# A tenth expert tile ahead of the router, a busier TensorE while it decides, and the last expert pair in another order

## The chip, the cores and the metric
The kernel runs on one core of one Trainium2 chip. Its time is the device time of one execution in microseconds. The core has five engines that run side by side and meet at semaphores: TensorE (PE; its weight loads are listed as PEld), VectorE (DVE), ScalarE (ACT), GpSimd (POOL) and SyncE (SP), which here mostly issues DMAs. On-chip memory is SBUF; TensorE writes its products to the eight banks of PSUM, B[0] to B[7], 128 partitions of 512 fp32 each.

## The reference
One block of a diffusion backbone over 512 latent tokens of width 1024, with 256 context tokens, all in fp32. First come a Hyena long convolution and an mLSTM side by side, with one output projection (not touched by the change). Then the expert-choice mixture of experts: 16 experts, each of which takes its 64 best tokens.

```
aff = softmax(h2 @ w_router)                # 512 x 16
g, idx = top_k(aff per expert, 64)
a, u  = xs @ w_gate, xs @ w_up              # per expert 64x1024 @ 1024x2048, twice
ye    = (silu(a) * u) @ w_down * g          # per expert 64x2048 @ 2048x1024
y2    = scatter-add of ye onto the 512 tokens
out   = x + g2 * rmsnorm(y2, post_norm2)
```

The weights of one expert are 24 MB (gate, up and down, 8 MB each), all 16 some 403 million bytes, each read once.

## The kernel before
**Tiles and ring.** An expert is cut into 12 tiles of 128 x 4096 fp32 (2048 KB): gate and up in four pairs (256 rows of the inner dimension each, q = 0 to 3), then four of down. Two experts make a pair, so a pair has 24 tiles in the order of `TILES`: g0 u0 g1 u1 g2 u2 g3 u3 d0 d1 d2 d3 of the first expert (tiles 0 to 11) and the same of the second (12 to 23). There are eight pairs. The tiles go to a ring of `NSLOT` = 8 places in SBUF. In the first pair tiles 0 to 7 fill the eight places and tile 8 goes to `yacc`, the 128 x 4096 tensor that later takes the sums; GpSimd clears it once the tile has been used (L503). From then on tile n takes the place of tile n - 8.

**SyncE's order** (L388 to L449). Its queue is in program order and a wait in it holds all that is behind. Tile 0 is issued when the last tile of the input projection has been used, tile 1 after the inverse transforms, tiles 2 and 3 after the mLSTM numerators, then the router weights (L421), tiles 4 to 6 when the output projection is done (`p_w`), tiles 7 and 8 when the logits are done (`p_lg`). Then each later tile waits (`used`) until TensorE has used the tile whose place it takes: tiles 9 to 16 wait for tiles 0 to 7, tile 17 for tile 9, tile 18 for tile 10 and so on.

**Routing** (TensorE L965 to L983, VectorE L1761 to L1795). After the logits: softmax, eight rounds of max and replace on VectorE for the 64 best, threshold, ranks by two small products, and the selection matrices. TensorE has a few small products in it and otherwise waits. Then it gathers the tokens of the first pair by products with the selection matrix (L998) and starts the experts.

**A pair on TensorE** (`expert_pair`, L1002): `gate_up(0)` into banks 0 to 3 (L1038, L1039), the scatter of the pair before it (`scatter`, L1104, two banks in turn, VectorE adds each half row of 512 to `yacc`, L1823), `turn(0, ...)` (transposes of the hidden activations), `down(0)` (L1062, bank 5), `gate_up(1)`, transposes of the affinity-weighted selection (L1081), gather for the next pair, `turn(1, ...)`, `down(1)`. ScalarE makes the silu (L1317), VectorE the product with up (L1830), ScalarE copies the results out (L1322). In the profile a 128x512 fp32 matmul is two records. The last pair has the same order, without the gather.

**Tail.** After `down(1)` of the last pair: copy of the results, eight scatters, each added on VectorE to `yacc`; then per 128 tokens the sum of squares and the root on ScalarE, reciprocal, product with the gate row and sum with the residual on VectorE. The first 128 tokens are finished by ScalarE and GpSimd (L507 to L510), the other three by VectorE (L1877 to L1880). Four output DMAs of 512 KB.

The working tensor `moe` (128 x 6144) holds the inner tensors of the experts from column 0: gathered tokens 0 to 1023, silu 1024 to 2047, hidden to 3071, turned hidden to 4095, results to 5119. Before that its columns serve the mLSTM and small tables of the router.

Of the kernel before, what the change touches and what calls it, by code (L numbers as in the profile page):

```python
# [16 lines left out]
ALU = mybir.AluOpType  # L17
# [4 lines left out]
P = 128  # L22
# [90 lines left out]
def block_kernel(nc, A, out):  # L113
    ctx = ExitStack()
    with ctx:
# [9 lines left out]
        def slot(n, a=0, b=SLOTF):  # L125
# [107 lines left out]
        hdt = moe[:, 3072:4096].rearrange("p (b n) -> p b n", b=2)  # L233
        ye = moe[:, 4096:5120]
# [4 lines left out]
        y3 = yacc[:, :].rearrange("p (c n) -> p c n", c=NLT)  # L239

# [19 lines left out]
        keep = moe[:, 1280:1280 + NSQ * E]  # L260
        mks = moe[:, 1424:1424 + NSQ * E]
# [3 lines left out]
        shp = moe[:, 1024:1152].rearrange("p (k e) -> p k e", k=KD)  # L265
        shs = moe[:, 1152:1168]
# [7 lines left out]
        d_extra = sem("d_extra")  # L274
# [8 lines left out]
                 "v_wra", "v_h2", "v_ry", "a_y0", "g_y0", "a_aft", "v_sub", "v_aft", "v_th", "v_mkt", "v_slot", "v_xs", "v_hid",  # L283
# [55 lines left out]
        def _(sp):  # L339
# [48 lines left out]
            def expert_tile(i, pair):  # L388
                kind, st = TILES[i]
# [4 lines left out]
                if i == NSLOT and first:  # L394
                    dst, loaded = yacc[:, :], d_extra
# [12 lines left out]
            def used(i, pair):  # L408

                kind, st = TILES[i]  # L410
                sp.wait_ge(S["p_dn" if kind == "d" else "p_gu"], 8 * pair + st + 1)
# [9 lines left out]
            sp.dma_start(wr.rearrange("p (a b) e -> p a (b e)", b=2), A["w_router"][0].rearrange("(a p b) e -> p a (b e)", p=P, b=2)).then_inc(d_wr, 16)  # L421
            sp.wait_ge(S["p_w"], len(DONE))
# [16 lines left out]
            for i in range(NTI - NSLOT):  # L439
                used(i, NPAIR - 1)  # L440
                expert_tile(i + NSLOT, NPAIR - 1)

            for c in (1, 2, 0, 3):
                if c:
                    sp.wait_ge(S["v_res"], c)
                else:
                    sp.wait_ge(S["g_y0"], 2)
                sp.dma_start(out[0, c * P:(c + 1) * P, :], y3[:, c, :]).then_inc(d_out, 16)
            sp.wait_ge(d_out, 16 * NLT)  # L449

        @block.gpsimd
        def _(pool):
# [53 lines left out]

            pool.wait_ge(S["a_y0"], 1)  # L507
            g.tensor_tensor(y3[:, 0, :], y3[:, 0, :], g2p[:, :], ALU.mult).then_inc(S["g_y0"], 1)
            pool.wait_ge(S["g_y0"], 1)
            g.tensor_tensor(y3[:, 0, :], y3[:, 0, :], x3[:, 0, :], ALU.add).then_inc(S["g_y0"], 1)  # L510

        @block.tensor
        def _(pe):
# [434 lines left out]

            rows_turned(0)
# [14 lines left out]
            logits(3)  # L964
            pe.wait_ge(S["v_aft"], 1)  # L965
# [6 lines left out]

            pe.wait_ge(S["v_th"], 1)
# [8 lines left out]
            mm(ranks, ones, before, start=False, stop=True).then_inc(S["p_rk"], 1)  # L982
            pe.wait_ge(S["v_slot"], 2)  # L983
# [18 lines left out]
            def expert_pair(jm, first, last):  # L1002

                def ring_tile(kind, st):
                    i = TILES.index((kind, st))
                    if first and i == NSLOT:
                        pe.wait_ge(d_extra, 16)
                        return yacc[:, :]
# [3 lines left out]
                    if not (first and i < NSLOT):  # L1012
                        count = count + (i - 1) // NSLOT
                    pe.wait_ge(d_ring[r], 16 * count)
                    return slot(SLOT_OF[r])

                def gate_up(e2):

                    for q in range(4):
                        wg = ring_tile("g", 4 * e2 + q).rearrange("p (k n) -> p k n", k=2)  # L1020
# [11 lines left out]
                        for k in range(2):  # L1032
                            lhs = xst[:, 2 * q + k, CAP * e2:CAP * (e2 + 1)]
                            for n in range(4):
                                cols = slice(n * CH, (n + 1) * CH)
                                flags = dict(start=(q == 0 and k == 0), stop=(q == 3 and k == 1))
# [13 lines left out]
                def down(e2):  # L1050

                    turned = S["v_hdt" if e2 else "a_hdt"]
                    for q in range(4):
# [6 lines left out]
                        for k in range(4):  # L1060
                            for half in range(2):
                                x = mm(B[5][CAP * half:CAP * (half + 1), :],  # L1062
                                       hdt[:, q // 2, k * P + at:k * P + at + CAP],
# [11 lines left out]
                turn(0, 1)  # L1075
                down(0)

                gate_up(1)
                pe.wait_ge(S["g_sel"], 2 * jm + 4)
                for c in range(NLT):  # L1080
                    x = tr(B[4][:, c * P:(c + 1) * P], pw[:, c, :], idn)  # L1081
                x.then_inc(S["p_pwt"], 1)
                if not last:
                    pe.wait_ge(S["v_sel"], 4 * jm + 12)
                    if not first:
                        pe.wait_ge(S["v_yacc"], 8 * jm + 8)
                    gather_half(jm, 1)
                pe.wait_ge(S["a_pwt"], jm + 2)
                turn(1, 0)
                if not last:  # L1090
                    gather_half(jm, 0)
                turn(1, 1)
                down(1)

# [17 lines left out]
            scatter(NPAIR - 1, range(2 * NLT))  # L1112

        @block.scalar
        def _(act):
# [195 lines left out]
            def expert_pair(j, last):  # L1311
# [6 lines left out]

                def results(e2):
                    act.wait_ge(S["p_dn"], 8 * j + 4 * e2 + 4)  # L1320
                    for half in range(2):
# [4 lines left out]
                for m in range(2):  # L1326
                    act.wait_ge(S["p_ht"], 4 * j + m + 1)
                    a.activation(hdt[:, m, :], B[3 if m else 4][:, :], ACT.Copy).then_inc(S["a_hdt"], 1)
                results(0)
# [572 lines left out]
```

## Time and profile before
| | us |
|---|---|
| runs | 1377.02, 1379.55, 1380.71; median 1379.55 |
| profiled execution | 1377.64, of which 1375.4 span |
| TensorE busy | 1230.3 (89%) |
| VectorE / ScalarE / GpSimd busy | 309.5 / 186.7 / 35.2 |
| DMA read from HBM | 453.53 MB |
| chain of waits: TensorE / DMA | 61% / 30% of the span |
| largest single entry of the chain | DMA ring<-in_w_exp_up, 28% |
| expert tiles, issue to landing (median) | 25.2 (gate), 27.9 (up), 27.0 (down) |

TensorE's busy time is a poor sign of what bounds this kernel: its records overlap and are modelled. The reader should look for who waits for whom in each stretch: before 410 us the projections and the two token mixers, 410 to 434 the routing, then the experts, and from 1350 the tail. The granted clock is given as a share of 2.4 GHz, 0.50 being 1.2 GHz.

### The profile page before, as it was taken

To read this page: it belongs to the slowest core of one execution; us is meant where nothing else is said; L and a number is where in the kernel's file an instruction comes from. 1 tells how busy PE (TensorE), PEld (TensorE's weight loads), DVE (VectorE), ACT (ScalarE), POOL (GpSimd) and SP (SyncE) were. 2 spreads that over 40 slices of the span, in tenths; PEclk is the share of its full clock that TensorE was granted. 3 is DMA by queue.
4 is the path that set the end of the run, shared out by engine and by line. 5 is a ranking of instruction groups with operands and counts; after the bars stand their busy time and mean duration, and the time that the engine had idled before them with its cause. 6 is when DMAs were issued, how large, how long until landed. Compare 5 with 4: busy or idle time off the path is not lost.

```text
span 1375.4 us, 12966 instructions
## 1 busy us (share of the span) xinstructions
PE 1230.3 (89%) x5360; PEld 534.3 (39%) x5360; DVE 309.5 (23%) x601; ACT 186.7 (14%) x377; POOL 35.2 (3%) x58
## 2 busy tenths in 40 slices
PE   6899999999996999989798988989989898897985
PEld 2444454456463334325234332423423433242331
DVE  3634301737333101201111020110102002010215
ACT  3400010013330101102001010100101101010102
POOL 2000010000000100000000000000000000000001
PEclk9999999999997999999999999999999999999998
DMA  9733422262216999999999999999999999999991
GB/s 352 274 122 122 147 97 94 91 243 99 89 71 280 425 428 428 427 428 427 427 429 429 428 428 428 430 428 428 428 428 430 428 428 428 428 432 426 427 417 63
DMA packets 44504, 456.08 MB, mean 332 GB/s; under 512 B 6048, under 2 KB 6160, under 8 KB 16570
## 3 DMA queue, kind: packets, MB, share of 16 engines
q1 hardware_dynamic: 43826, 455.46, 79.3%
q8 instruction: 23, 0.38, 0.1%
q10 hardware_dynamic: 264, 0.11, 0.0%
q0 software_dynamic: 384, 0.07, 0.0%
q14 instruction: 7, 0.06, 0.0%
HBM read 453.53 MB, written 2.10 MB: 331 GB/s over the span
## 4 chain that ended last, share of the span: by engine, by line
PE 61%; DMA 30%; DVE 5%; issue 2%; ACT 2%; SPq 1%; DVEq 0%; ACTq 0%
DMA ring<-in_w_exp_up 28%; PE B L1062 16%; PE B L666 6%; PE B L1038 6%; PE B L1039 6%; PE B L899 4%; PE B L990 4%; PE B L758 3%; PE B L1104 2%; PE B L825 2%; PE B L716 2%; DMA ring<-in_pos 2%; PE B L1047 1%; PE B L576 1%; PE B L615 1%
## 5 line engine op out<-in xcount | busy, mean ns | idle before, releaser
L1038 PE MATMUL B<-ring,moe 128*64 128x512 f32 x1024 | 468.8, 612 | 78.2 <-DMA ring<-in_w_exp_up 65.6
L1039 PE MATMUL B<-ring,moe 128*64 128x512 f32 x1024 | 467.3, 613 | 0.0
L1038 PEld LDWEIGHTS B<-ring,moe 128*64 128x64 f32 x1024 | 141.0, 141 | 234.9 <-issue 213.6
L1062 PE MATMUL B<-ring,moe 128*64 128x512 f32 x1008 | 220.6, 595 | 0.0
L1830 DVE TENSOR_TENSOR moe<-moe,B 64x512 f32<-64x512 f32 x64 | 43.8, 685 | 734.3 <-ACT moe L1317 733.0
L1039 PEld LDWEIGHTS B<-ring,moe 128*64 128x64 f32 x1024 | 140.9, 141 | 146.3 <-issue 146.3
L1062 PEld LDWEIGHTS B<-ring,moe 128*64 128x64 f32 x1008 | 71.1, 137 | 138.2 <-issue 136.2
L1317 ACT ACTIVATE moe<-B 64x512 f32<-64x512 f32 x64 | 37.9, 592 | 503.5 <-PE B L1039 502.3
L666 PE MATMUL B<-ring 128*128 128x512 f32 x192 | 84.1, 595 | 0.0
L1104 PE MATMUL B<-moe 128*128 128x512 f32 x128 | 64.4, 618 | 9.8 <-DVE yacc L1823 7.9
L990 PE MATMUL B<-moe,xl 128*128 128x128 f32 x448 | 55.0, 281 | 0.0
L990 PEld LDWEIGHTS B<-moe,xl 128*128 128x128 f32 x448 | 53.9, 196 | 0.0
L666 PEld LDWEIGHTS B<-ring 128*128 128x128 f32 x192 | 35.9, 190 | 45.9 <-issue 45.8
L1322 ACT ACTIVATE moe<-B 64x512 f32<-64x512 f32 x32 | 18.9, 592 | 244.5 <-PE B L1062 244.1
L1823 DVE TENSOR_TENSOR yacc<-yacc,B 128x512 f32<-128x512 f32 x64 | 43.8, 684 | 29.1 <-PE B L1104 28.7
L758 PE MATMUL B<-ring 128*128 128x512 f32 x96 | 41.8, 593 | 0.0
L1104 PEld LDWEIGHTS B<-moe 128*128 128x128 f32 x128 | 20.9, 189 | 48.2 <-DVE yacc L1823 34.6
L899 PE MATMUL B<-ring,fr 128*128 128x512 f32 x64 | 28.4, 597 | 0.2 <-ACT fr L1265 0.2
L825 PE MATMUL B<-ring 128*128 128x512 f32 x64 | 28.4, 597 | 0.0
L716 PE MATMUL B<-ring 128*128 128x512 f32 x64 | 28.1, 596 | 0.0
L899 PE MATMUL B<-ring 128*128 128x512 f32 x64 | 28.0, 592 | 0.0
L758 PEld LDWEIGHTS B<-ring 128*128 128x128 f32 x96 | 18.0, 190 | 22.4 <-issue 22.4
(303 smaller groups left out, 790.8 us busy)
## 6 DMA issues: line engine op xcount, KB each, us to landing
ring<-in_w_exp_gate SPq DMA_DIRECT2D x64, 2048.0 KB, 25.2
ring<-in_w_exp_up SPq DMA_DIRECT2D x64, 2048.0 KB, 27.9
ring<-in_w_exp_down SPq DMA_DIRECT2D x63, 2048.0 KB, 27.0
ring<-in_w_mod SPq DMA_DIRECT2D x12, 2048.0 KB, 8.2
ring<-in_w_in SPq DMA_DIRECT2D x6, 2048.0 KB, 7.9
ring<-in_w_out SPq DMA_DIRECT2D x2, 2048.0 KB, 7.8
xl<-in_x SPq DMA_DIRECT2D x1, 2048.0 KB, 21.6
ring<-in_pos SPq DMA_DIRECT2D x1, 2048.0 KB, 26.1
```

The lines of the kernel that those rows point to most:

```text
L666: x = mm(B[b][:, :], w[:, k, m * P:(m + 1) * P], ht[:, k, LC:], start=(k == 0), stop=(k == KD - 1))
L716: x = mm(B[b][:, :], w[:, k, m * P:(m + 1) * P], ht[:, k, LC:], start=(k == 0), stop=(k == KD - 1))
L758: x = mm(B[b][:, :], ht[:, k, t * P:(t + 1) * P], w[:, k, :], start=(k == 0), stop=(k == KD - 1))
L825: x = mm(B[b][:, :], ht[:, k, LC + c * P:LC + (c + 1) * P], w[:, k, :], start=(k == 0), stop=(k == KD - 1))
L899: x = mm(B[b][:, :], lhs, wo[half][:, k, :], start=(k == 0), stop=(k == KD - 1))
L990: x = mm(B[6 + g][:, k * P:(k + 1) * P], x3[:, c, pair_rows(dk)], psel[:, c, :], start=(c == 0), stop=(c == NLT - 1))
L1038: mm(gate, lhs, wg[:, k, cols], **flags)
L1039: x = mm(up, lhs, wu[:, k, cols], **flags)
L1062: x = mm(B[5][CAP * half:CAP * (half + 1), :], hdt[:, q // 2, k * P + at:k * P + at + CAP], wd[:, k, half * CH:(half + 1) * CH], start=(q ...
L1104: mm(B[6 + half][:, :], pwt[:, c, :], ye[:, half * CH:(half + 1) * CH], start=True, stop=True).then_inc(S["p_sca"], 1)
L1823: v.tensor_tensor(dst, dst, B[6 + half][:, :], ALU.add).then_inc(S["v_yacc"], 1)
L1830: v.tensor_tensor(hid[o, n // 2, :], sil[o, n // 2, :], B[n][o, :], ALU.mult).then_inc(S["v_hid"], 1)
```

## The change
- **Tenth tile.** `OWN_HOME` gives two tiles of the first pair a place of their own: tile 7 in columns 1024 to 5119 of `moe`, tile 8 in `yacc`. Tile 7 is issued right behind the router weights, once the mLSTM's last readers of these columns are done (`p_num` 16, `v_hn` 4); tile 9 is issued with tile 8 after the logits, into the place that tile 7 had. Tiles 10 to 16 wait for tiles 0 to 6, tile 17 for tile 9 as before. The router's small tables move from `moe` to `fr`.
- **keep_busy.** 128x512 products whose result nobody reads: one before the wait for the softmax, seven before the wait for the threshold, two before the wait for the slots.
- **Last pair.** Order `LAST`: the 16 gate and up tiles first, then the eight down tiles. The second expert's turned hidden goes to its own columns (`hdl`). Within `gate_up(1)` TensorE turns the selection and puts `yacc` into PSUM by products with the identity (`accumulator`), half row by half row; the rest of these follow later.
- **Tail.** The scatters accumulate in eight banks on top of that; nothing is added on VectorE. ScalarE squares straight from PSUM, VectorE multiplies with the gate row from PSUM and ends each 128 tokens with one fused operation. VectorE copies half of the last results. GpSimd has no part. The last 128 tokens leave in two DMAs.

```
+        OWN_HOME = {NSLOT - 1: moe[:, 1024:5120], NSLOT: yacc[:, :]}
+        LAST = [t for t in TILES if t[0] != "d"] + [t for t in TILES if t[0] == "d"]
+        SCATTER_BANK = [6, 7, 0, 1, 2, 4, 3, 5]
-            return i if first and i < NSLOT else (i - 1) % NSLOT
+            return i if first and i < NSLOT - 1 else (i - 2) % NSLOT
...
             sp.dma_start(wr.rearrange(...), ...).then_inc(d_wr, 16)
+            sp.wait_ge(S["p_num"], NH * NLT)
+            sp.wait_ge(S["v_hn"], NLT)
+            expert_tile(NSLOT - 1, 0)
             sp.wait_ge(S["p_w"], len(DONE))
             expert_tile(4, 0)
             expert_tile(5, 0)
             expert_tile(6, 0)
             sp.wait_ge(S["p_lg"], NLT)
-            expert_tile(7, 0)
             expert_tile(NSLOT, 0)
-            for i in range(NSLOT):
+            expert_tile(NSLOT + 1, 0)
+            for i in range(NSLOT - 1):
                 used(i, 0)
-                expert_tile(i + NSLOT + 1, 0)
+                expert_tile(i + NSLOT + 2, 0)
...
+            def keep_busy(b, n):
+                take(b)
+                for _ in range(n):
+                    mm(B[b][:, :], idn, cst[:, 0:CH], start=True, stop=True)
             logits(3)
+            keep_busy(0, 1)
             pe.wait_ge(S["v_aft"], 1)
...
+            keep_busy(0, 7)
             pe.wait_ge(S["v_th"], 1)
...
+            keep_busy(2, 2)
             pe.wait_ge(S["v_slot"], 2)
...
+                if last:
+                    gate_up(1)
+                    pe.wait_ge(S["a_pwt"], jm + 2)
+                    turn(1, 0)
+                    accumulator(2)
+                    accumulator(3)
+                    turn(1, 1)
+                    down(0)
+                    down(1)
+                    return
...
+            def accumulator(n):
+                c, half = divmod(n, 2)
+                mm(B[SCATTER_BANK[n]][:, :], idn, y3[:, c, half * CH:(half + 1) * CH], start=True, stop=False)
...
-            scatter(NPAIR - 1, range(2 * NLT))
+            pe.wait_ge(S["a_ye"], 4 * NPAIR - 1)
+            for n in range(2 * NLT):
+                c, half = divmod(n, 2)
+                if n == 1:
+                    pe.wait_ge(S["v_ye"], 1)
+                if n in (4, 6):
+                    accumulator(n)
+                    accumulator(n + 1)
+                mm(B[SCATTER_BANK[n]][:, :], pwt[:, c, :], ye[:, half * CH:(half + 1) * CH],
+                   start=False, stop=True).then_inc(S["p_sca"], 1)
...
+            for n in range(2 * NLT):
+                c, half = divmod(n, 2)
+                act.wait_ge(S["p_sca"], 8 * (NPAIR - 1) + n + 1)
+                a.activation(sil[:, half, :], B[SCATTER_BANK[n]][:, :], ACT.Square,
+                             accum_out=(sy if half else ss2)[:, c:c + 1]).then_inc(S["a_sy"], 1)
...
+            def gated(c):
+                for half in range(2):
+                    n, h = 2 * c + half, slice(half * CH, (half + 1) * CH)
+                    dve.wait_ge(S["a_sy"], 2 * NLT + n + 1)
+                    link(v.tensor_tensor(y3[:, c, h], B[SCATTER_BANK[n]][:, :], g2p[:, h], ALU.mult))
+            def result(c):
+                dve.wait_ge(S["a_fsd"], c + 1)
+                link(v.reciprocal(ry[:, c:c + 1], sd2[:, c:c + 1]))
+                for h in (slice(0, D),) if c < NLT - 1 else (slice(0, CH), slice(CH, D)):
+                    stt(y3[:, c, h], y3[:, c, h], ry[:, c:c + 1], x3[:, c, h], ALU.mult, ALU.add).then_inc(S["v_res"], 1)
+            gated(0)
+            for c in range(1, NLT):
+                gated(c)
+                result(c - 1)
+            result(NLT - 1)
```

## Rows read from the trace of the kernel before

**Rows 1.** Windows: start:end, length, five engines busy, PEclk, DMA share, GB/s.

```profile
410.00:432.00 22.00, 8.71 (x38) 7.58 (x39) 13.19 (x47) 2.56 (x6) 1.98 (x3) 0.50 0.98 417
...
430.00:435.00 5.00, 5.00 (x31) 4.72 (x31) 0.73 (x2) 0.25 (x1) 0.00 (x0) 0.70 0.29 125
...
480.00:1340.00 860.00, 770.89 (x3576) 309.77 (x3574) 106.92 (x184) 84.67 (x146) 10.25 (x21) 0.98 1.01 428
...
1340.00:1342.00 2.00, 2.00 (x12) 0.70 (x10) 0.00 (x0) 0.00 (x0) 0.00 (x0) 1.00 0.31 131
```

**Rows 2.** Waits of TensorE from 441 to 1345: us in total, times, longest.

```profile
PE B L1038 <- DMA ring<-in_w_exp_up: 65.6, 31, 3.9
```

**Rows 3.** Timeline of SyncE: start us, us (several merged), queue, line, what.

```profile
363.92 0.38 SPq L421 DMA_DIRECT2D ring<-in_w_router  x1
405.35 0.33 SPq L406 DMA_DIRECT2D ring<-in_w_exp_gate  x1
...
412.99 0.33 SPq L406 DMA_DIRECT2D ring<-in_w_exp_up  x1
...
441.77 9.43 SPq L406 DMA_DIRECT2D ring<-in_w_exp_down  x3
...
479.77 0.33 SPq L406 DMA_DIRECT2D ring<-in_w_exp_up  x1
...
493.51 7.67 SPq L406 DMA_DIRECT2D ring<-in_w_exp_down  x4
```

**Rows 4.** Timeline of TensorE in the routing and the first gathers.

```profile
424.37 0.28 PE L975 MATMUL B<-cst_sb,fr 16*128 16x16 f32 x1 [8.46 <-DVE fr L1784]
...
428.85 5.87 PE L998 MATMUL B<-moe,xl 128*128 128x128 f32 x32 [2.42 <-issue]
...
441.66 2.15 PE L998 MATMUL B<-moe,xl 128*128 128x128 f32 x16
```

**Rows 5.** Timeline of TensorE behind the first silu pause.

```profile
471.38 4.92 PE L1062 MATMUL B<-yacc,moe 128*64 128x512 f32 x16
```

**Rows 6.** Timeline of the last pair, TensorE and VectorE.

```profile
1264.69 0.61 PE L1038 MATMUL B<-ring,moe 128*64 128x512 f32 x1 [3.89 <-DMA ring<-in_w_exp_up]
...
1283.41 13.95 PE L1062 MATMUL B<-ring,moe 128*64 128x512 f32 x64
...
1330.69 0.65 PE L1081 MATMUL B<-cst_sb,fr 128*128 128x128 f32 x4
1331.43 2.83 DVE L1830 TENSOR_TENSOR moe<-moe,B 64x512 f32<-64x512 f32 x4 [47.70 <-ACT moe L1317]
...
1333.93 1.94 PE L1047 MATMUL B<-cst_sb,moe 128*128 128x128 f32 x8 [2.58 <-ACT moe L1332]
...
1335.80 14.80 PE L1062 MATMUL B<-ring,moe 128*64 128x512 f32 x64
```

**Rows 7.** Chain of waits: start us, us, engine, line.

```profile
1281.29 1.72 PE B L1104 x4
```

**Rows 8.** Timeline of the tail.

```profile
1350.64 1.21 ACT L1322 ACTIVATE moe<-B 64x512 f32<-64x512 f32 x2 [16.77 <-PE B L1062]
1351.99 7.67 PE L1104 MATMUL B<-moe 128*128 128x512 f32 x16 [1.40 <-ACT moe L1322]
1353.13 0.69 DVE L1823 TENSOR_TENSOR yacc<-yacc,B 128x512 f32<-128x512 f32 x1 [16.53 <-PE B L1104]
...
1371.15 1.23 DVE L1880 TENSOR_TENSOR yacc<-yacc,xl 128x1024 f32<-128x1024 f32 x1
```

**Rows 9.** The tile yacc in the tail: ns min/median/max, first and last start.

```profile
L1366 DVE SCALAR_TENSOR_TENSOR yacc<-yacc,col,g2p x3: 1284/1285/3224, 1360.6 to 1369.8; 128x1024 f32<-128x1024 f32 x3
...
DMA to landing us min/median/max: 2.6/2.7/3.6
```

**Rows 10.** Timeline of ScalarE in the first norm (squares of two half rows).

```profile
386.41 0.59 ACT L1282 ACTIVATE moe<-B 128x512 f32<-128x512 f32 x1
...
387.45 0.60 ACT L1282 ACTIVATE moe<-B 128x512 f32<-128x512 f32 x1
```

More of the change, by code:

```diff
@@ L406, in expert_tile, with used @@
                 sp.dma_start(dst, src).then_inc(loaded, 16)
-            def used(i, pair):
-                kind, st = TILES[i]
+            def used(i, pair, order=TILES):
+                kind, st = order[i]
                 sp.wait_ge(S["p_dn" if kind == "d" else "p_gu"], 8 * pair + st + 1)
@@ L439, in _ @@
             for i in range(NTI - NSLOT):
[L440 to L447, printed above, removed]
-                sp.dma_start(out[0, c * P:(c + 1) * P, :], y3[:, c, :]).then_inc(d_out, 16)
-            sp.wait_ge(d_out, 16 * NLT)
+                used(i, NPAIR - 1, LAST)
+                expert_tile(i + NSLOT, NPAIR - 1, LAST)
+            for c in range(NLT - 1):
+                sp.wait_ge(S["v_res"], c + 1)
+                sp.dma_start(out[0, c * P:(c + 1) * P, :], y3[:, c, :]).then_inc(d_out, 16)
+            for half in range(2):
+                h = slice(half * CH, (half + 1) * CH)
+                sp.wait_ge(S["v_res"], NLT + half)
+                sp.dma_start(out[0, (NLT - 1) * P:L, h], y3[:, NLT - 1, h]).then_inc(d_out, 16)
+            sp.wait_ge(d_out, 16 * (NLT + 1))
         @block.gpsimd
@@ L1004, in ring_tile, with weights_turned @@
                 def ring_tile(kind, st):
[L1005 to L1008, printed above, removed]
+                    i = (LAST if last else TILES).index((kind, st))
+                    if first and i in OWN_HOME:
+                        pe.wait_ge(d_own[i], 16)
+                        return OWN_HOME[i]
                     r = ring_slot(i, first)
                     count = NTI // NSLOT * jm + NTI // NSLOT + 1
-                    if not (first and i < NSLOT):
-                        count = count + (i - 1) // NSLOT
+                    if not (first and i < NSLOT - 1):
+                        count = count + (i - 2) // NSLOT
                     pe.wait_ge(d_ring[r], 16 * count)
                     return slot(SLOT_OF[r])
+                def weights_turned():
+                    pe.wait_ge(S["g_sel"], 2 * jm + 4)
+                    for c in range(NLT):
+                        x = tr(B[4][:, c * P:(c + 1) * P], pw[:, c, :], idn)
+                    x.then_inc(S["p_pwt"], 1)
                 def gate_up(e2):
                     for q in range(4):
+                        if last and e2 == 1 and q == 1:
+                            pe.wait_ge(S["v_yacc"], 8 * jm + 8)
+                            weights_turned()
+                        if last and e2 == 1 and q in (2, 3):
+                            accumulator(q - 2)
                         wg = ring_tile("g", 4 * e2 + q).rearrange("p (k n) -> p k n", k=2)
@@ L1052, in down @@
                     turned = S["v_hdt" if e2 else "a_hdt"]
+                    src = hdl if last and e2 else hdt
                     for q in range(4):
@@ L1317, in silu, with weights_turned @@
                         a.activation(sil[o, n // 2, :], B[n][i, :], ACT.Silu).then_inc(S["a_sil"], 1)
+                def weights_turned():
+                    act.wait_ge(S["p_pwt"], j + 1)
+                    a.activation(pwt, B[4][:, :].rearrange("p (c n) -> p c n", c=NLT), ACT.Copy).then_inc(S["a_pwt"], 1)
                 def results(e2):
                     act.wait_ge(S["p_dn"], 8 * j + 4 * e2 + 4)
-                    for half in range(2):
+                    for half in range(1 if last and e2 else 2):
                         a.activation(ye[CAP * e2:CAP * (e2 + 1), half * CH:(half + 1) * CH],
```

85 lines of the change are left out of this document (39 added, 46 removed).

## The prediction

> **What bounds the kernel now.** I read the windows first. From 480 to 1340 us the DMA share is 1.01 at 428 GB/s with the granted clock at 0.98 [rows 1]. An expert tile is 2.097 MB, so one tile costs 2.097/0.428 = 4.90 us, and that stream of 183 tiles sets the pace. The waits of TensorE say the same: from 441 to 1345 it waited 65.6 us for ring tiles [rows 2], some 9 us in each of seven expert pairs of 24 x 4.90 = 117.6 us. Three places are not the stream: the stretch in front of it, where the DMA stands still, the last pair, where TensorE sets the end, and the tail.
>
> In front: SyncE issues tiles 4 to 6 at 405.35 and tiles 7 and 8 at 412.99 and then has no free place until TensorE has used tiles 0 and 1, at 441.77 [rows 3]. The window 430 to 435 moved 125 GB/s x 5 = 0.62 MB, so the five tiles ended at 431.5; 5 x 4.90 = 24.5 us before that is 406.9, so data start 1.6 us after an issue. The DMA idles from 431.5 to about 443.4. Meanwhile TensorE's clock is 0.50, that is 1.2 GHz, from 410 to 432 [rows 1]: little work had been on it, and the first 32 gather records take 5.87 us, where 16 later take 2.15 [rows 4].
>
> At the end: data stop at 1340.6 (131 GB/s x 2 us in the window from 1340, [rows 1]), but TensorE works on tiles 20 to 23 without a pause from 1335.80 to 1350.64 [rows 6, 8]. The last stretch is 1350.64 to the span's end at 1375.4, 24.8 us, with no expert work.
>
> **Change, part 1: the tenth tile.** Tile 7 goes to its own place and is issued right behind the router weights at 363.92 [rows 3], into a stretch with no transfers, so its 4.9 us cost nothing. Tiles 8 and 9 are issued where 7 and 8 were. 182 tiles are left for the stream where 183 were: worth 4.9 us if nothing else is late. But something is. From tile 17 on the old rule holds: tile n is issued when n-8 is used, and tile 17 needs tile 9 used, in the first down product: issued at 479.77 [rows 3]. Before, tile 16 ended at 443.4 + 8 x 4.90 = 482.6, so 479.77 + 1.6 = 481.4 was early by 1.2 us. With one tile fewer ahead of it, the queue is empty earlier, and tile 17 can start only 1.2 us earlier than before, whatever was won in front of it, unless TensorE uses tile 9 sooner. So the tenth tile alone is worth 1.2 us, not 4.9.
>
> **Part 2: the keep_busy matmuls.** A 128x512 product is two records of 0.43 us (4 records in 1.72, [rows 7]): 0.87 us at 2.4 GHz, 1.74 at 1.2 GHz. One stands before the wait for the softmax, seven before the threshold (released at 424.37, with TensorE idle 8.5 us), two before the wait for the slots [rows 4]. Their cover: 7 cost 6.1 us at full clock; the stretches at low clock that follow an idle spell ended after 3.3 to 4.2 us of work (428.85 to some 433 is one, [rows 4]), so at worst 6.1 + 2 = 8.1 < 8.5. If the clock stayed low they cost 12.2 us and the threshold comes 3.7 us late. I take: hidden, and the first gather at full clock: 5.87 - 4.2 = 1.7 us, and the small products of the ranking win another 0.4. So tile 9 is used 2.1 us sooner: issue of tile 17 at 477.7, start 479.3 instead of 482.6. Bounds: 0 (clock down again by 428.85) and 2.1; or -3.7.
> Parts 1 and 2 together: 1.2 + 2.1 = 3.3 us. Tile 10 would be issued at 439.7, tiles 10 to 16 end at 441.3 + 7 x 4.90 = 475.6, and the DMA then idles 3.7 us. Tile 20 is issued 13.7 us behind tile 17 (493.51 before), where the data of 17 to 19 need 14.7, and 18 and 19 come at even steps between: no second hole. The stream is full from there, so the 3.3 us reach tile 7 of the last pair.
>
> **Part 3: the last pair's order.** Before: TensorE gets that tile at 1264.69 and starts the first down product at 1283.41, 18.7 us later [rows 6]. After: 1261.4 and 1280.1, and there gate and up of the second expert begin (their tiles 8 and 9 have landed by then). Four times 6.9 us (half of the 13.95 us that 64 records take), plus 0.65 for the transposes moved in, plus two accumulator products, 1.7: 1310.0. From the last gate/up record to the first turn, 2.2 us of silu and hidden (1331.43 + 1.4 - 1330.7; before it was 3.3, since the turn also waited for the copy of the weights, which is now long done). Turns, two more accumulators and the first down product: 0.5 + 1.7 + 0.5 + 13.9 = 16.7 us, and 1.7 for a clock that falls in the pause, as it did at 1333.93 (8 records in 1.94 us, then 14.80 where 13.95 would do): 1330.7. The second down product writes the same bank: it waits for two copies, 1.4 us as from 1350.64 to 1351.99 [rows 8]. Then 13.9: **1346.0**, 4.6 us less than 1350.64. Tile 23 landed at about 1264.6 + 16 x 4.90 = 1343.0, now at 1339.7, and is reached at 1342.5, so TensorE, not the DMA, sets this end. The floor is 1339.7 + 3.5 = 1343.2; with an undisturbed clock 1344.3. So the new order is worth 1.3 us by itself; 3.3 come from parts 1 and 2.
>
> **Part 4: the tail,** from the last down record = 0. ScalarE copies one half (0.6), VectorE the other beside it; the first scatter starts at 0.8 instead of 1.35. TensorE needs 8 scatters and 4 accumulators, 12 x 0.87; a consumer starts 1.14 after its scatter's start [rows 8]; scatters 6 and 7 are there at 10.6 and 11.5. ScalarE: 1.04 us for a first half with its small Identity, 0.71 for a second, 0.3 for the root, as in the first norm's rows [rows 10]: squares of 7 end at 12.4. VectorE per 128 rows: two products of 0.69, reciprocal 0.2, one fused 1.28 us operation [rows 9]. Its last block: product 7 from 12.4 to 13.1; result(2) to 14.6; reciprocal, two halves of 0.7: 16.2. Last issue there; before, the span ended 3.0 us after the last VectorE operation (1371.15 + 1.23 to 1375.4). So 19.2, or 18.6 if the smaller last transfer is quicker by its 0.26 MB at 428 GB/s. I take 19.0 against 24.8: **5.8 us**. What goes is the adding on VectorE and two of its operations at 3.2 us instead of 1.28 (the median and the longest in [rows 9]), which lay beside GpSimd's work on the same tile. Bounds: a clock that falls adds 1.7, one that stays low some 9; with result(2) wholly ahead of product 7, 12.4 + 0.7 + 0.2 + 1.4 + 3.0 = 17.7.
>
> One rule weighs against the split of the last output. The row: a 512 KB output lands 2.7 us after its issue, median [rows 9]. The Trainium skill (DMA: Bandwidth & Descriptors, "Anatomy of one DMA") has a fixed part of about 2.0 us in each DMA, whatever its size; by it the half would land 2.0 + 0.26/0.428 = 2.6 us after its issue, an estimate, and with both fixed parts in a row the split would win nothing: the tail would be 19.2 by it at the worst and 18.6 at the best. It moves neither the case nor a chance.
>
> **Sum.** 3.3 + 1.3 + 5.8 = 10.4 us of the profiled execution's 1377.64: 1367.2. The four times shown (1377.02, 1377.64, 1379.55, 1380.71) have their mean at 1378.7 and the runs' median is 1379.55; I carry the gain to the mean: **1368.3 us**, with 1365.5 to 1371.5 as the likeliest case's own range.
>
> **Rivals.**
> A, the tenth tile pays fully (0.13): tile 9 is used in time, because the clock does not fall in the first silu pause. For it: the cost there is only the 4.92 us for 16 records where 3.5 would do [rows 5]. Tile 17 then starts 1.5 us sooner; to have all 4.9 + 2.1 = 7.0 us TensorE would have to be 3.7 us quicker. 1364.6 to 1366.8.
> B, the kept clock is not kept (0.17): it is low again at the gather, and 2.1 us go: 1370.4; or the seven run at 1.2 GHz throughout and the threshold is 3.7 us late: 10.4 - 5.8 = 4.6 us gained, 1374.1. Against the latter: no stretch of steady work stayed low beyond 4.2 us.
> C, the tail is not shorter (0.10): three accumulator products or a semaphore round trip per half take what the fused operations bring, so that only 4.6 + 1 remain: 1373.
> D, slower (0.05): TensorE at 1.2 GHz from the pause at 1310 through both down products. It has 30.6 us of full-speed work there, which would become 61.2: 1368.3 + 29 = 1397. It decides against the change only from 29 us at low clock on (10.4 + 4.1 = 14.5 us lost); the stretch at 1333.93 got its clock back in under 4 us.
> E, it doesn't do what it says: tile 7 would be late because SyncE waits for the normed heads; but the router load behind the same VectorE work is at 363.92. Under 0.01.
> The forecast has 0.55.
>
> **Numbers.** What a measurement of this kernel can tell from no change is 0.3%, 4.1 us: faster means under 1375.4, slower over 1383.7. Forecast, A, the most of B and of C are faster: 0.87; same 0.08; slower 0.05. Range 1363.5 to 1375.
>
> **What would show it.** Tile 7's load near 364; clock 1.00 at the gather, gather 4.2 us; the first reused place issued near 439.7; a DMA hole of 3 to 4 us near 476; last down record near 1346; no hole in the last pair; 19 us from it to the end. It would be wrong if there is no hole and 7 us come through, if the clock is 0.5 at the gather, or if the last output is issued over 17.5 us behind the last down record.

## The result and the profile after

The changed kernel takes 1366.61 us (median of 4 runs, 1364.18 to 1367.61); the kernel before, beside it, 1380.13 (4 runs). The ratio is 0.9904, 95% interval 0.9887 to 0.9921: 13.3 us faster (10.9 to 15.6), where 10.4 were forecast. The profiled execution of after took 1367.61 us with a span of 1365.6, against 1377.64 and 1375.4: 10.0 us between these two executions, 9.8 between their spans. The time alone does not say which case of the prediction came: 1366.61 lies in the forecast's own range (1365.5 to 1371.5) and in that of rival A (1364.6 to 1366.8). The profile does.

The windows of after (columns as in [rows 1]):

```profile
410.00:432.00 22.00, 19.33 (x69) 11.42 (x68) 13.91 (x48) 3.71 (x7) 1.99 (x3) 0.80 1.00 426
...
470.00:474.00 4.00, 4.00 (x13) 1.27 (x14) 0.79 (x2) 0.60 (x1) 0.00 (x0) 0.57 1.01 430
474.00:478.00 4.00, 4.00 (x22) 1.29 (x18) 0.00 (x0) 0.00 (x0) 2.62 (x1) 1.00 0.69 291
478.00:482.00 4.00, 4.00 (x20) 1.29 (x18) 0.00 (x0) 0.00 (x0) 1.03 (x2) 1.00 0.57 168
480.00:1340.00 860.00, 777.79 (x3598) 313.93 (x3596) 106.87 (x184) 86.15 (x148) 10.23 (x20) 0.98 1.00 427
1336.00:1338.00 2.00, 2.00 (x12) 0.77 (x10) 0.00 (x0) 0.00 (x0) 0.00 (x0) 1.00 0.77 328
1338.00:1340.00 2.00, 2.00 (x12) 0.78 (x10) 0.00 (x0) 0.00 (x0) 0.00 (x0) 1.00 0.12 49
```

Three things are to be seen. The clock over the routing is 0.80 instead of 0.50. The stream has the hole that was forecast: 291 and 168 GB/s where 427 is full, so (136 + 259)/427 x 4 = 3.7 us are missing between 474 and 482. And data stop near 1338, TensorE is at work behind them.

SyncE's issues in after, to be held against [rows 3]:

```profile
365.16 0.44 SPq L412 DMA_DIRECT2D moe<-in_w_exp_up  x1
406.11 0.33 SPq L412 DMA_DIRECT2D ring<-in_w_exp_gate  x1
...
414.14 0.33 SPq L412 DMA_DIRECT2D yacc<-in_w_exp_down  x1
...
478.79 0.33 SPq L412 DMA_DIRECT2D ring<-in_w_exp_up  x1
```

Tile 7 leaves at 365.16. Tile 17 (478.79) is 72.7 us behind tile 4 (406.11), where it was 74.4; tile 4 itself leaves 0.8 us later in this execution, which no part of the change explains (its issue varies from 405.1 to 407.2 over all kernels here).

TensorE in the routing, the last pair and the tail of after (timeline, to [rows 4, 6, 8]):

```profile
416.85 7.22 PE L958 MATMUL B<-cst_sb 128*128 128x512 f32 x14
...
425.52 0.22 PE L988 MATMUL B<-cst_sb,fr 16*128 16x16 f32 x1 [1.45 <-DVE fr L1845]
...
429.63 4.01 PE L1012 MATMUL B<-moe,xl 128*128 128x128 f32 x32 [0.69 <-issue]
...
1312.93 0.94 PE L1074 MATMUL B<-cst_sb,moe 128*128 128x128 f32 x4 [2.22 <-DVE moe L1891]
...
1313.66 3.37 PE L1131 MATMUL B<-yacc,cst_sb 128*128 128x512 f32 x4
...
1332.75 13.95 PE L1090 MATMUL B<-ring,moe 128*64 128x512 f32 x64 [1.36 <-issue]
1346.74 0.59 ACT L1373 ACTIVATE moe<-B 64x512 f32<-64x512 f32 x1 [14.09 <-PE B L1090]
...
1361.28 1.41 DVE L1427 SCALAR_TENSOR_TENSOR yacc<-yacc,col,xl 128x512 f32<-128x512 f32 x2
```

The seven idle products end 1.45 us before the threshold, the gather takes 4.01 us, the turn in the last pair is at low clock (0.94 us for four records; 0.63 at full clock), the second down product waits 1.36 us, and the last down record ends near 1346.7.

### The profile page after: what moved, and what is told of

Read it like the earlier page. It is cut to its first block, busy times and chain, and to the rows that moved or that the text cites. A ratio compares the mean times of both kernels' runs of the same rounds, so it can differ in the third digit from the quotient of the medians.

```text
span 1365.6 us, 13064 instructions
## 1 busy us (share of the span) xinstructions
PE 1245.3 (91%) x5396; PEld 542.2 (40%) x5396; DVE 304.2 (22%) x601; ACT 187.5 (14%) x388; POOL 29.7 (2%) x56
## 4 chain that ended last, share of the span: by engine, by line
PE 65%; DMA 26%; DVE 4%; issue 2%; ACT 1%; SPq 1%; DVEq 0%; ACTq 0%
DMA ring<-in_w_exp_up 24%; PE B L1090 16%; PE B L1065 8%; PE B L1066 7%; PE B L671 6%; PE B L904 4%; PE B L1004 4%; PE B L763 3%; PE B L830 2%; PE B L721 2%; DMA ring<-in_pos 2%; PE B L1142 2%; DVE moe L1891 1%; PE B L1074 1%; PE B L581 1%
## 5 line engine op out<-in xcount | busy, mean ns | idle before, releaser
L1142 PE MATMUL B<-moe 128*128 128x512 f32 x112 | 56.7, 619 | 8.4 <-DVE yacc L1884 7.9
L1884 DVE TENSOR_TENSOR yacc<-yacc,B 128x512 f32<-128x512 f32 x56 | 38.3, 684 | 10.8 <-PE B L1142 10.4
```

Of the source, the lines that this page charges most:

```text
L1142: mm(B[6 + half][:, :], pwt[:, c, :], ye[:, half * CH:(half + 1) * CH], start=True, stop=True).then_inc(S["p_sca"], 1)
L1884: v.tensor_tensor(dst, dst, B[6 + half][:, :], ALU.add).then_inc(S["v_yacc"], 1)
```

## A ruler for all profiles

Five marks cut every kernel in the same way: the issue of tile 4 (a), the issue of tile 17 (b), the landing of the last pair's tile 7 (c), the copy behind the last down record (d), the end of the span (e). A sixth, the first issue behind the logits (l), is needed because a is a loose mark: from a to l it is 6.5 to 8.0 us, in kernels that have the same instructions there too. From l on the routing sets when TensorE uses the first tile, so what lies between a and l is to be taken off before two kernels are compared. All numbers are in us.

| profile | a | a to l | a to b | a to c | c to d | d to e |
|---|---|---|---|---|---|---|
| before | 405.35 | 7.64 | 74.42 | 859.20 | 86.09 | 24.76 |
| before_again | 407.24 | 7.98 | 75.52 | 858.76 | 88.00 | 24.80 |
| no_pool | 405.63 | 7.82 | 73.94 | 858.76 | 85.94 | 23.37 |
| end_only | 405.44 | 6.53 | 72.75 | 857.75 | 85.69 | 18.82 |
| no_busy | 406.74 | 8.04 | 74.07 | 856.25 | 83.84 | 18.87 |
| nine | 406.75 | 8.03 | 72.67 | 855.97 | 83.88 | 18.90 |
| after | 406.11 | 8.03 | 72.68 | 854.92 | 85.71 | 18.86 |
| again | 405.14 | 8.03 | 72.68 | 854.90 | 85.72 | 18.84 |
| front_only | 406.80 | 6.95 | 71.59 | 853.94 | 85.72 | 24.74 |
| old_order | 405.35 | 7.65 | 73.05 | 855.40 | 90.86 | 18.89 |
| swap | 406.07 | 7.07 | 68.22 | 855.01 | 83.75 | 18.87 |
| bank_pause | 406.86 | 8.03 | 72.67 | 854.82 | 83.12 | 18.90 |
| first_pause | 405.67 | 7.64 | 71.34 | 853.59 | 83.79 | 18.85 |
| best | 405.61 | 7.65 | 69.64 | 854.96 | 83.21 | 17.92 |

Taken from l, mark c lies at 850.8 to 851.6 in the four kernels with the old front (before, before_again, no_pool, end_only; mean 851.1) and at 846.8 to 847.0 in after, again, front_only and bank_pause. That is 4.2 us, and within 0.8 and 0.2 us it repeats.

## The experiments

The theory is the prediction's. The main rival is that a tile more ahead is worth a tile of the stream, 4.9 us. The times of no_busy, swap, first_pause, bank_pause and best have 95% intervals that overlap those of the changed kernel (0.9887 to 0.9921 and 0.9886 to 0.9917), so what each edit does is read from its profile, and each of these is one execution.

**no_busy**: the three calls removed.

```
-            keep_busy(0, 1)
...
-            keep_busy(0, 7)
...
-            keep_busy(2, 2)
```

> The changed kernel without its ten idle products. Theory (tile 17 waits for tile 9, so what TensorE wins before the gather passes through, and the tenth tile is worth 1.2 us): gather of 32 records near 5.9 us at clock 0.5 instead of 4.0, tile 17 issued 2.1 us later against the router weights' issue (116.2 us behind it instead of 114.1), the DMA hole in front of tile 17 stays 3 to 4 us, time 2.1 us over the changed kernel. Rival (the products only fill idle time, the queue makes up for it): time within 0.5 us of the changed kernel, because the DMA has ten tiles in hand.

Measured: 1367.47 us, ratio 0.9918 (0.9904 to 0.9933). The gather took 6.73 us, more than expected, but the silu pause that follows then left the clock alone. The windows of no_busy:

```profile
470.00:474.00 4.00, 1.74 (x10) 1.31 (x12) 3.72 (x8) 2.66 (x6) 0.00 (x0) 1.00 1.01 430
...
478.00:482.00 4.00, 4.00 (x22) 1.40 (x20) 0.00 (x0) 0.00 (x0) 3.06 (x2) 1.00 0.89 315
482.00:486.00 4.00, 4.00 (x22) 1.33 (x20) 0.00 (x0) 0.00 (x0) 0.00 (x0) 1.00 0.81 319
```

Tile 17 comes 1.4 us later from tile 4 on (74.07 against 72.68) and the hole is (112 + 108)/427 x 4 = 2.1 us instead of 3.7. The stream ends 1.35 us later in the ruler, not 2.1, and the times cannot tell it from the changed kernel. So the idle products are worth 1.35 us in this pair of profiles, half of the 2.7 us that they win at the gather; the other half is the clock, which fell in the first silu pause of again and not in that of no_busy. That is not a rule: in before, before_again, no_pool and end_only, which have no idle products either, it fell in both places. On nine tiles the products are worth more: nine against the four kernels with the old front has 3.2 us from l to c.

**nine**: nine tiles ahead, idle products kept.

```
-        OWN_HOME = {NSLOT - 1: moe[:, 1024:5120], NSLOT: yacc[:, :]}
+        OWN_HOME = {NSLOT: yacc[:, :]}
```

(with SyncE's order and the ring's count as in the kernel before.)

> The changed kernel with nine tiles ahead as before, idle products kept. Theory: no DMA hole before tile 17, which starts 1.2 us later than in the changed kernel, so only 1.2 us are lost. Rival (a tile ahead is worth a tile of the stream): 4.9 us lost.

Measured: 1368.98 us, ratio 0.9930 (0.9915 to 0.9944). No hole:

```profile
474.00:478.00 4.00, 4.00 (x22) 1.42 (x20) 0.00 (x0) 0.00 (x0) 1.98 (x1) 0.99 1.02 430
478.00:482.00 4.00, 4.00 (x22) 1.36 (x20) 0.00 (x0) 0.00 (x0) 1.66 (x2) 1.00 0.99 422
```

Tile 17 is issued at the same distance (72.67 and 72.68), and mark c comes 1.07 us later (855.97 against 854.90): the 1.2 that was forecast. That refutes the rival's 4.9 us where the idle products are kept. The times alone would not: nine's ratio is 0.0028 above that of the changed kernel (0.9930 against 0.9904 and 0.9901), some 4 us, with intervals that overlap.

**end_only** and **front_only**: the two halves of the change, made by the same edits.

> The changed kernel with nine tiles and no idle products: only the last pair's order and the tail are new. Theory: 1.3 + 5.8 = 7.1 us under the kernel before, 3.3 us over the changed one; last down record some 1.3 us earlier than before, 19 us from it to the end instead of 24.8. Rival (the front brings most): 4 us or less under the kernel before.

> The kernel before with the tenth tile and the idle products, last pair and tail as before. Theory: 3.3 us under the kernel before, a DMA hole of 3 to 4 us before tile 17. Rival (tile ahead worth a tile): 4.9 + 2.1 = 7 us under it. Second rival (front gain is lost because the last pair is set by TensorE): 0 to 1 us.

Measured: end_only 1369.75 us, 0.9938 (0.9924 to 0.9953), 8.6 us under the kernel before; front_only 1373.89 us, 0.9962 (0.9948 to 0.9976), 5.2 us under it. They add up to 13.8, the whole change gave 13.3: within the noise no part hides another. Both halves gave more than expected (7.1 and 3.3), and the rivals of end_only (4 or less) and the second of front_only (0 to 1) did not come; the interval of front_only, 3.3 to 7.2 us, leaves open by itself whether 3.3 or 7 is right. The front's gain is in the ruler from a to c (853.94, 1.0 us under after, because a to l is 1.1 us shorter), the end's in d to e. From c to d front_only and after are equal (85.72 and 85.71), although after also puts the sums into PSUM there.

**again**: the changed kernel.

> The changed kernel once more, on the chip of the three runs beside it. Both accounts of the size: if 10.4 us (0.9925) is the true gain and the first figure scatter, the ratio comes out near 0.992 to 0.993; if something unseen helps, near 0.990 again.

Measured: 1366.63 us, 0.9901 (0.9886 to 0.9917). The 13 us are real; they are not the scatter of four runs.

**before_again**: the kernel before.

> The kernel before once more, for a second profile of it. The gain in the times is 13.5 us where the two first profiles show 10.0. Theory (the first profile of before was a quick one, by clock and start): this profile lies near 1379.5, with the extra 2 us in front of the experts or in the stretches at low clock. Rival (the profiles are typical and the times differ outside the span): again 1377.6 with the same span.

Measured: 1379.62 us, 1.0003 (0.9994 to 1.0013); its profiled execution took 1380.97, with a span of 1378.8. Its timeline shows where 3.4 us more come from without any change. The last pair of before_again, and beside it that of before:

```profile
1315.10 0.61 PE L1038 MATMUL B<-ring,moe 128*64 128x512 f32 x1 [2.57 <-DMA ring<-in_w_exp_up]
1324.89 1.09 PE L1038 MATMUL B<-ring,moe 128*64 128x512 f32 x1 [2.70 <-DMA ring<-in_w_exp_up]
```

```profile
1313.86 1.09 PE L1038 MATMUL B<-ring,moe 128*64 128x512 f32 x1 [2.71 <-DMA ring<-in_w_exp_up]
1323.67 0.61 PE L1038 MATMUL B<-ring,moe 128*64 128x512 f32 x1 [1.16 <-DMA ring<-in_w_exp_up]
```

Tile 4 left 1.9 us later (mark a), and c to d took 1.9 us more. The clock is low equally often from c to d in both; what differs is where. In before it fell behind the first of two waits for a tile (the first product takes 1.09 us there and 0.61 at full clock), and the second wait was the shorter for it, 1.16 us. In before_again it fell behind the second, with no wait left to make up for it. From this profile to that of again it is 14.2 us: 2.1 to mark a, 3.9 in the stream, 2.3 in the last pair, 6.0 in the tail. The first profile of before was a quick one (1377.64 us, 2.5 under the median beside the changed kernel), and this one is slow by 1.4 us (1380.97 against its median of 1379.62).

**swap**: the place that tile 17 waits for is used one tile sooner.

```
-        OWN_HOME = {NSLOT - 1: moe[:, 1024:5120], NSLOT: yacc[:, :]}
+        OWN_HOME = {NSLOT - 1: moe[:, 1024:5120], NSLOT + 1: yacc[:, :]}
...
-                used(i, 0)
+                used(NSLOT if i == NSLOT + 1 else i, 0)
...
-            pool.wait_ge(S["p_dn"], 1)
+            pool.wait_ge(S["p_dn"], 2)
...
```

> The changed kernel, but tile 9 goes to yacc and tile 8 to the ring place, so that tile 17 waits for tile 8, which the first down product uses one tile earlier; GpSimd clears yacc one tile later. Theory (the hole is TensorE's use of the ring tile in the first down product): tile 17 issued 3.4 us sooner, hole of 3.7 us nearly gone, the rest of the kernel 3.4 us earlier. Rival (the DMA is bound elsewhere, the hole is filled later anyway): hole gone, time unchanged within 1 us.

Measured: 1364.79 us, 0.9887 (0.9870 to 0.9904). The expectation failed. Tile 17 did leave sooner, by 4.5 us from a (68.22) and by 3.5 from l, where 3.4 were expected, but mark c came no sooner: at the same distance from a (855.01), and 1.1 us later from l. The last expert tile of all landed 926.7 us behind l, as in again (926.6). The windows of swap:

```profile
474.00:478.00 4.00, 4.00 (x22) 1.32 (x20) 0.00 (x0) 0.00 (x0) 0.24 (x1) 1.00 0.99 381
478.00:482.00 4.00, 4.00 (x22) 1.35 (x20) 0.00 (x0) 0.00 (x0) 3.40 (x2) 1.00 0.74 307
482.00:486.00 4.00, 4.00 (x20) 1.26 (x18) 0.00 (x0) 1.19 (x2) 0.00 (x0) 1.00 0.98 328
```

The hole is not filled but spread: 46, 120 and 99 GB/s are missing in these three windows, 2.5 us, and another 0.7 from 490 to 498 (381 and 397 GB/s). One place comes free sooner, but the next ones, of tiles 10, 11 and 13, come free when TensorE gets there, which has not changed: tile 18 leaves 52.5 us behind the start of the gather (481.16 less 428.63), in after 52.6 (482.22 less 429.63). What its median has under that of again is in the last pair (83.75 against 85.72), where the edit does nothing and the clock stayed up.

**first_pause**: two more idle products in the first pair's silu pause.

```
                 if first:
+                    for _ in range(2):
+                        mm(B[6][:, :], idn, cst[:, 0:CH], start=True, stop=True)
                     turn(0, 0)
```

> The changed kernel with two more idle products in the first silu pause of the first pair (into bank 6). Theory (TensorE's use of tile 9 sets the restart of the stream): the clock stays at 1.00 from 470 to 474, tile 17 is issued 1.3 to 1.7 us sooner against the threshold, the hole shrinks by as much, the last pair's tile 7 lands as much sooner. Rival (as the moved tile 8 suggested, a shorter hole comes back as smaller ones): the first hole is shorter, tile 7 of the last pair lands within 0.5 us of before.

Measured: 1363.93 us, 0.9889 (0.9873 to 0.9904). The windows of first_pause:

```profile
470.00:474.00 4.00, 4.00 (x20) 1.37 (x22) 0.71 (x2) 0.58 (x1) 0.39 (x1) 1.00 1.01 426
474.00:478.00 4.00, 4.00 (x20) 1.29 (x18) 0.00 (x0) 0.00 (x0) 3.25 (x2) 1.00 0.73 291
478.00:482.00 4.00, 4.00 (x22) 1.34 (x20) 0.00 (x0) 0.00 (x0) 0.00 (x0) 1.00 0.94 336
```

Clock 1.00 instead of 0.57, tile 17 1.3 us sooner, hole (136 + 91)/427 x 4 = 2.1 us instead of 3.7, and mark c comes 1.3 us sooner (853.59 against 854.91). Unlike in swap, all that TensorE uses from here on comes sooner, and the gain stays to the end. The edit itself won more than that. In this execution the clock fell once ahead of the gather, under the last two idle products of the routing (timeline of first_pause):

```profile
426.35 3.44 PE L958 MATMUL B<-cst_sb 128*128 128x512 f32 x4
```

In after they took 1.88 us. The gather began 0.8 us later for it (16.3 us behind l instead of 15.5), so that against the threshold tile 17 is only 0.9 us sooner, under the 1.3 to 1.7 expected; from the start of the gather both tile 17 and mark c are 1.8 us sooner. The other part of the median's 2.7 us under again is the last pair (83.79 against 85.72), where the edit does nothing.

**old_order**: the last pair's tiles in the old order, all else as changed.

```
-        LAST = [t for t in TILES if t[0] != "d"] + [t for t in TILES if t[0] == "d"]
+        LAST = TILES
...
+                    down(0)
                     gate_up(1)
                     pe.wait_ge(S["a_pwt"], jm + 2)
                     turn(1, 0)
                     accumulator(2)
                     accumulator(3)
                     turn(1, 1)
-                    down(0)
                     down(1)
...
```

> The changed kernel with the last pair's tiles in the old order (first down product before the second gate and up), accumulators and tail as changed. Theory: the order is worth 1 to 2 us, as TensorE and not the DMA sets the last down record; last down record some 1.5 us later than in the changed kernel. Rival (the order brings the greater part of the end's 7 us, because it lets TensorE catch up with the stream): 4 us or more lost.

Measured: 1371.44 us, 0.9930 (0.9913 to 0.9947), and c to d 90.86 us, 5.1 more than again. The rival (4 us or more) came, not the theory. The timeline and a window of old_order show why:

```profile
1309.84 0.61 PE L1065 MATMUL B<-ring,moe 128*64 128x512 f32 x1 [0.76 <-DMA ring<-in_w_exp_up]
...
1320.79 1.08 PE L1065 MATMUL B<-ring,moe 128*64 128x512 f32 x1 [2.81 <-DMA ring<-in_w_exp_up]
...
1333.09 0.73 PE L1074 MATMUL B<-cst_sb,moe 128*128 128x128 f32 x4 [2.22 <-DVE moe L1891]
...
1333.64 3.58 PE L1131 MATMUL B<-yacc,cst_sb 128*128 128x512 f32 x4
...
1337.61 13.95 PE L1090 MATMUL B<-ring,moe 128*64 128x512 f32 x64
```

```profile
1319.00:1327.00 8.00, 6.21 (x16) 2.10 (x18) 0.00 (x0) 0.00 (x0) 0.00 (x0) 0.57 1.01 428
```

In the old order TensorE waits for two up tiles behind c, 0.76 and 2.81 us; in after it waits for none, but 1.36 us for bank 5, which old_order does not. That is 2.2 of the 5.1 us. The rest is the clock, 0.57 from 1319 to 1327 where after has 1.00: it follows the second wait, but how much of it a second profile would show is open (the six runs lie between 1367.76 and 1374.45). The four accumulator products ahead of the last down product are in both. In the old order two of them stand behind the last wait for a tile, where nothing makes up for them; with them, and with the clock low once more, old_order took 4.8 us more from c to d than before. In the new order they cost nothing against the kernels without them: before waits 3.9 us for two tiles there and its clock falls behind the first of these waits, after waits for none, and after took as long as front_only (85.71 and 85.72), 0.4 us less than before (86.09) and 2.3 less than before_again (88.00).

**bank_pause**: TensorE's chain in the last pair shortened.

```
+                    bank = B[2] if last and e2 else B[5]
...
-                        if last and e2 == 1 and q in (2, 3):
-                            accumulator(q - 2)
...
                     gate_up(1)
+                    accumulator(0)
+                    accumulator(1)
...
```

> The changed kernel with two edits in the last pair: the second down product writes bank 2, so it need not wait for the copies out of bank 5, and the accumulators 0 and 1 stand in the silu pause instead of between gate and up tiles. Theory (TensorE's own chain sets the end): 1.4 us of the bank wait, 1.7 us of accumulators hidden in the pause of 2.2 us, up to 1.7 us of low clock go, last down record 3 to 4.5 us earlier, limited by the last tile's landing (about 3.3 us before the last down record now). Rival (the last tile's landing sets it): last down record less than 1 us earlier.

Measured: 1364.83 us, 0.9885 (0.9869 to 0.9900); c to d 83.12, 2.6 us less, where 3 to 4.5 were expected. The timeline of bank_pause:

```profile
1336.33 3.65 PE L1089 MATMUL B<-ring,moe 128*64 128x512 f32 x16 [1.34 <-DMA ring<-in_w_exp_down]
1341.10 3.65 PE L1089 MATMUL B<-ring,moe 128*64 128x512 f32 x16 [1.11 <-DMA ring<-in_w_exp_down]
```

Now TensorE waits for the last two tiles: the floor is reached, 3.7 us behind the last landing. In after it was TensorE that was late, as forecast. Of the 2.6 us some 1.9 is the clock, which stayed up in the filled pause; nine, no_busy, swap and first_pause, where it stayed up in the empty one, have 83.8 to 83.9.

**no_pool**: the kernel before with GpSimd out of the tail.

```
-            g.tensor_tensor(y3[:, 0, :], y3[:, 0, :], g2p[:, :], ALU.mult).then_inc(S["g_y0"], 1)
...
-            for c in range(1, NLT):
+            for c in range(NLT):
```

> The kernel before, but the first 128 tokens of the tail are finished by VectorE like the others, and GpSimd and ScalarE have no part in it. Theory (VectorE's 3.2 us operations lie beside GpSimd's): every such operation takes 1.2 to 1.3 us, VectorE ends 10.8 us behind the last root of 1360.3, that is near 1371.1 instead of 1372.4: 1 to 1.5 us faster although VectorE does a quarter more. Rival (the long ones are late for another reason, such as the output DMAs): they stay long and the time grows by 2.5 us.

Measured: 1376.82 us, 0.9986 (0.9975 to 0.9998), d to e 23.37 instead of 24.8. The tile yacc in its tail, to be held against [rows 9]:

```profile
L1357 DVE SCALAR_TENSOR_TENSOR yacc<-yacc,col,g2p x4: 1283/1285/1285, 1360.2 to 1368.1; 128x1024 f32<-128x1024 f32 x4
```

The longest is 1285 ns where it was 3224. The timeline of before has what lay beside it:

```profile
1363.02 2.34 POOL L508 TENSOR_TENSOR yacc<-yacc,g2p 128x1024 f32<-128x1024 f32 x1 [147.72 <-ACT yacc L1353]
...
1363.21 3.22 DVE L1366 SCALAR_TENSOR_TENSOR yacc<-yacc,col,g2p 128x1024 f32<-128x1024 f32 x1
1365.44 3.20 POOL L510 TENSOR_TENSOR yacc<-yacc,xl 128x1024 f32<-128x1024 f32 x1
1366.47 3.25 DVE L1880 TENSOR_TENSOR yacc<-yacc,xl 128x1024 f32<-128x1024 f32 x1
```

The two long operations of VectorE are the two that run beside GpSimd's. In no_pool VectorE does four blocks instead of three and still ends 1.4 us sooner behind d (20.36 us instead of 21.74). So 1.4 of the tail's 5.9 us come from GpSimd's leaving. That the rest comes from the adding and the second pass, which are gone, is argued; no run has one without the other.

**best**: swap and bank_pause together, and accumulators 5 and 6 in the waits for the last two tiles.

```
+                        if last and e2 and q in (2, 3):
+                            accumulator(q + 3)
```

> Everything that the experiments point to: tile 9 in yacc and tile 8 in the ring, second down product in bank 2, accumulators 0 and 1 in the silu pause, 5 and 6 in the waits for the last two tiles (1.3 and 1.1 us). Theory: last tile's landing sets the last down record, 3.7 us behind it; 0.5 us from the places, 2.5 us from the last pair, 0.6 us from the tail against the changed kernel: 1363, ratio 0.987 to 0.988. Rival (gains of the same stretch): no more than the bank and pause alone, 1364.8.

Measured: 1363.70 us, 0.9887 (0.9870 to 0.9904). The tail fell to 17.92, c to d is that of bank_pause (83.21 and 83.12), and swap's part gave nothing (854.96); in this execution the clock was low for longer in the first silu pause (0.61 from 466 to 470 and 0.54 from 470 to 474), so that tile 17 left later than in swap (69.64 against 68.22). Against again 2.9 us by the medians. It beats the kernel before clearly; that it beats the changed one is likely (the intervals, 0.9870 to 0.9904 and 0.9886 to 0.9917, overlap), and it cannot be told from first_pause and bank_pause, which have one aim each. first_pause with bank_pause was not run.

## Why the prediction was right

- **Part 1, the tenth tile, 1.2 us and not 4.9.** Right on top of the idle products: 1.07 us between nine and again, and a hole of 3.7 us, the forecast size, at the forecast place. Without them (no_busy against the four kernels with the old front) the tenth tile brought 2.9 us from l to c, or 2.0 with the 0.9 us of the third point below taken off. There the clock did not fall in the first silu pause, the condition of rival A, for which the prediction names 1.5 us more: 1.2 + 1.5 = 2.7. So the 1.2 holds for a clock that falls there, and that it fell in after was the likelier case, not a certain one.
- **Part 2, idle products.** Hidden, as forecast (1.45 us to spare), the gather at 4.01 us. Their worth was put at 2.1 us. It was 1.35 on ten tiles, where no_busy happened to keep its clock in the next pause, and on nine 3.2, or 2.3 without the same 0.9. In first_pause and old_order the last two of them ran at low clock and the gather began 0.8 us later: rival B came in part.
- **Parts 1 and 2 together, 3.3 us.** 4.2 us from l to c. The stream itself gained what was forecast: summed over the packets of the traces, the four kernels with the old front had moved 421.4 to 421.6 MB when that tile had landed, those with the new one 421.1 to 421.2. The difference, 0.37 MB or 0.9 us of stream, had gone to tiles behind it, and 4.2 - 0.9 = 3.3. Why the old front has more of the later tiles under way at c is open.
- **Data 1.6 us behind an issue.** The first packet of a tile starts 0.95 us behind its issue (405.35 and 441.77 in before). The 1.6 us is the start of an equal stream at full rate; the prediction uses it on both sides, and the sum does not change.
- **Part 3, the last pair, last down record at 1346.0.** It ended near 1346.7: low clock in the pause (0.94 us for four records) and the wait on bank 5 (1.36 us) were both there, and TensorE waited for no tile behind c. From the first to the last gate and up record of the second expert it took 30.8 us (1279.87 to 1310.71), where the prediction counts 30.0. The worth of the new order, 1.3 us, was measured at 0.4 us against the first profile, 2.3 against the second and 0.0 against front_only.
- **Part 4, the tail, 19.0 against 24.8.** 18.86 against 24.76. A 512 KB output landed 2.6 us behind its issue and a half of 256 KB 2.5 us, where the prediction estimates 2.6 from a section on DMAs that GpSimd issues; these are issued by SyncE. The smaller last transfer thus brings 0.1 to 0.2 us.
- **The sum.** 10.4 us forecast, 10.0 between the two first profiles, 13.5 between the medians. The parts are read from the profile of before, and its execution was 2.5 us under the median beside the changed kernel (1377.64 against 1380.13), that of after 1.0 over its own (1367.61 against 1366.61): 10.0 + 2.5 + 1.0 = 13.5. The prediction allowed for the first in part, by carrying the gain to the mean of four times, 1378.7. The nearness of 10.4 to 10.0 owes something to luck, for against before_again the same parts give 12.1 (14.2 less the 2.1 to mark a). The changed kernel's marks differ by 1.0 us between its two profiles in a, and by 0.02 in the other columns; its runs spread as widely as those of before (1364.53 to 1368.31 in again, 1378.48 to 1382.96 beside it).
- **Rivals.** A did not come: there is a hole, and the clock fell in the first silu pause of after as in before. C and D did not come.

## What to carry to other kernels

When a stream of transfers has a hole in front of it, find the first buffer whose release is set by compute: a deeper lead is worth only the distance to that point, and time won in the compute before it passes through (1.8 of 1.8 us in first_pause). Moving one release forward did nothing where the releases behind it stayed; moving them all did. A low clock, or a product added, cost little here where a wait for a transfer followed it, and much more behind the last such wait. And before a sum read from one profiled execution is carried to a median, take a second profile: here the same program's spans were 3.4 us apart, a quarter of the gain.

## What the runs showed of the hardware

- A silu pause of the same length did not always lower TensorE's clock. In the last pair c to d was 85.7 us in after, again and end_only and 83.8 to 83.9 in no_busy, nine, swap and first_pause, with the same instructions and a pause of 2.22 us in all seven; the windows 1312 to 1316 show 0.66 and 0.57 in after and again, 1.00 in nine, no_busy, swap and first_pause. In the four that kept the clock the first product behind c took 1.08 us, at low clock already; in the other three it took 0.61 us. Why is open.
- With two idle 128x512 products in such a pause it stayed at 1.00 (first_pause, 470 to 474: 1.00 for 0.57), and so it did with two accumulator products (bank_pause and best, last pair). This is three profiles, and no_busy kept 1.00 in the first silu pause with nothing in it, so that the products are the cause is likely, not shown.
- A gather that began at low clock took 5.87, 5.27 and 6.73 us in before, before_again and no_busy for the same 32 records, the longer the later the clock came back; 3.8 to 4.0 us in those that had idle products before it.
- VectorE's operation of 128x1024 with two SBUF inputs took 3.22 us beside a GpSimd operation (before) and 1.28 without (no_pool). The Trainium skill (GPSIMD Engine Reference, "Specifications") says that GpSimd's SBUF interfaces are shared with VectorE and contend with its instructions of two SBUF inputs; the trace agrees, with a factor of 2.5.
